# A step of the products between any two engines' parts of a layer norm, in seven of the twelve

## What is computed

```python
x <- LN0(alpha*x + 0.5*SwiGLU_1(x))
x <- LN1(alpha*x + Mix_l(x))          # layer 0: attention || retention; layer 1: S5 state-space model
x <- LN2(alpha*x + 0.5*SwiGLU_2(x))

def layer_norm(x, g, b):
    mu = jnp.mean(xf, -1, keepdims=True)
    var = jnp.mean(jnp.square(xf - mu), -1, keepdims=True)
    return (xf - mu) * lax.rsqrt(var + LN_EPS) * g + b

def swiglu(x, w_gate, w_up, w_down):
    return (jax.nn.silu(x @ w_gate) * (x @ w_up)) @ w_down
```

## Time and profile before

| | us |
|---|---|
| median of 3 runs | 2601.13 |
| lowest and highest | 2600.61, 2606.46 |
| the profiled execution | 2604.88 |
| its span, first to last instruction | 2603.2 |
| mean granted TensorE clock in it | 0.975 of full |

### The profile page before, as it was taken

How to read it: one execution, slowest core, us unless ns; L and a number is a source line. 1 busy time by engine, 2 the same in 40 slices (tenths; PEclk the granted TensorE clock), 3 DMA queues, 4 the chain that set the end, 5 groups by cost and what they waited for, 6 DMA issues and landing times.

```text
span 2603.2 us, 45460 instructions
## 1 busy us (share of the span) xinstructions
PE 2446.0 (94%) x18347; PEld 2295.4 (88%) x18347; DVE 1638.9 (63%) x2564; ACT 1085.3 (42%) x1645; POOL 470.4 (18%) x544
## 2 busy tenths in 40 slices
PE   6998899999899799999999999999999989989998
PEld 6998798998798667779889999999999888989997
DVE  5887766656765445567676657457656675577555
ACT  3433345333544223353254433555433536354333
POOL 5878600002100021200110202021001010121000
PEclk8999999999999999999999999999999999999999
DMA  7667666444354687644456455554555556545553
GB/s 173 175 188 196 164 194 194 131 117 121 114 151 120 211 250 234 172 120 134 119 155 186 149 155 174 173 170 137 155 153 146 170 171 200 154 139 154 147 153 93
DMA packets 676274, 417.26 MB, mean 160 GB/s; under 512 B 31554, under 2 KB 639682, under 8 KB 676066
## 3 DMA queue, kind: packets, MB, share of 16 engines
q1 hardware_dynamic: 669538, 393.98, 52.6%
q0 software_dynamic: 6528, 20.37, 2.6%
HBM read 395.51 MB, written 18.78 MB: 159 GB/s over the span
## 4 chain that ended last, share of the span: by engine, by line
PE 71%; DVE 15%; ACT 4%; issue 4%; DMA 2%; POOL 2%; SPq 1%; POOLq 0%; DVEq 0%; ACTq 0%
PE ps L256 19%; PE ps L257 18%; PE ps L258 18%; DVE w_lo L251 4%; ACT w_hi L242 2%; PE ps L864 2%; PE ps L865 2%; PE ps L866 2%; PE ps L2224 1%; PE ps L1559 1%; DVE h_lo L427 1%; PE ps L1574 1%; PE ps L1052 1%; DVE rstd L512 1%; PE ps L1601 1%
## 5 line engine op out<-in xcount | busy, mean ns | idle before, releaser
L251 DVE TENSOR_TENSOR w_lo<-w_raw,w_hi 128x1024 fp32r<-128x1024 f32 (+1 forms) x648 | 829.6, 1286 | 657.5 <-ACT w_hi L242 653.9
L256 PE MATMUL ps<-x_hi,w_hi 128*128 128x256 f32 (+1 forms) x3200 | 969.6, 303 | 51.0 <-DVE w_lo L251 48.2
L257 PE MATMUL ps<-x_lo,w_hi 128*128 128x256 f32 (+1 forms) x3200 | 955.4, 299 | 0.0
L258 PE MATMUL ps<-x_hi,w_lo 128*128 128x256 f32 (+1 forms) x3200 | 955.0, 298 | 0.0
L242 ACT ACTIVATE w_hi<-w_raw 128x1024 fp32r<-128x1024 f32 (+1 forms) x648 | 668.4, 1033 | 498.5 <-PE ps L258 353.1
L256 PEld LDWEIGHTS ps<-x_hi,w_hi 128*128 128x128 f32 x3200 | 615.5, 192 | 69.5 <-DVE w_lo L251 57.2
L257 PEld LDWEIGHTS ps<-x_lo,w_hi 128*128 128x128 f32 x3200 | 615.7, 192 | 1.4 <-issue 0.2
L258 PEld LDWEIGHTS ps<-x_hi,w_lo 128*128 128x128 f32 x3200 | 615.3, 192 | 0.0
L256 PE MATMUL ps<-h_hi,w_hi 128*128 128x256 f32 (+1 forms) x1408 | 425.2, 302 | 9.7 <-DVE w_lo L251 7.4
L257 PE MATMUL ps<-h_lo,w_hi 128*128 128x256 f32 (+1 forms) x1408 | 415.5, 295 | 0.0
L258 PE MATMUL ps<-h_hi,w_lo 128*128 128x256 f32 (+1 forms) x1408 | 415.2, 295 | 0.0
(11 more groups left out here) (263 smaller groups left out, 2282.8 us busy)
## 6 DMA issues: line engine op xcount, KB each, us to landing
w_raw<-in_ffn_w_gate SPq DMA_DIRECT2D x176, 512.0 KB, 4.3
w_raw<-in_ffn_w_up SPq DMA_DIRECT2D x176, 512.0 KB, 3.9
w_raw<-in_ffn_w_down SPq DMA_DIRECT2D x128, 512.0 KB, 3.9
w_raw<-in_w_in_ab SPq DMA_DIRECT2D x56, 512.0 KB, 4.1
w_raw<-in_ffn_w_down SPq DMA_DIRECT2D x64, 384.0 KB, 3.2
arena<-in_cache_v POOLq DMA_DIRECT2D x64, 256.0 KB, 4.4
arena<-in_cache_k SPq DMA_DIRECT2D x64, 256.0 KB, 3.9
w_raw<-in_w_out_ab SPq DMA_DIRECT2D x16, 512.0 KB, 3.7
```

What stands on the lines that cost most here:

```text
L251: dve.tensor_tensor(T.w_lo[:, u % RING, 0:n], T.w_raw[:, u % RAW, 0:n], T.w_hi[:, u % RING, 0:n].bitcast(F32), ALU.subtract).then_inc(T.w_ ...
L256: pe.matmul(out, w_hi, m_hi, start=first, stop=False)
L257: pe.matmul(out, w_hi, m_lo, start=False, stop=False)
L258: return pe.matmul(out, w_lo, m_hi, start=False, stop=last)
```

## The change

`Norm` takes a number `slack`. With 0 everything stays at its step; with 1 each engine's part moves one more step away from the part of another engine that it waits for, and the norm has 12 steps: squares and their sums in 2 and 3 (from 1 and 2), variance in 5 (from 4), root in 6 (from 4), reciprocal and scaling in 7 and 8 (from 5 and 6), rounding in 8 and 9 (from 5 and 6), `x_lo` in 9 and 10 (from 6 and 7), bias in 10 and 11 (from 7 and 8). N0A, N1A, N2A, N1B, N4A, N4B and N5A get `slack=1`. `STEPS` itself goes from 10 to 9. Nothing happened in the tenth step, but `norm_and_s5`, `beside_a` and `beside_b` count from `Norm.STEPS - 2`, so the S5 part of both groups begins one norm step earlier, in the product step of the norm's last scaling.

```diff
 class Norm:
-    STEPS = 10
+    STEPS = 9
 
-    def __init__(self, T, g, row, scale, products, alone=False):
+    def __init__(self, T, g, row, scale, products, alone=False, slack=0):
 
-        self.alone = alone
+        self.alone, self.steps, n = alone, self.STEPS + 3 * slack, slack
+        self.square_at, self.var_at, self.root_at = 1 + n, 4 + n, 4 + 2 * n
+        self.scale_at, self.round_at, self.rest_at, self.bias_at = 5 + 2 * n, 5 + 3 * n, 6 + 3 * n, 7 + 3 * n
...
     def vector(self, dve):
         T = self.T
-        for i in range(self.STEPS):
+        for i in range(self.steps):
...
-            if i in (5, 6):
-                for k in range(4 * i - 20, 4 * i - 16):
+            if i in (self.scale_at, self.scale_at + 1):
+                for k in self.half(i, self.scale_at):
...
-            if i in (1, 2):
-                for k in range(4 * i - 4, 4 * i):
+            if i in (self.square_at, self.square_at + 1):
+                for k in self.half(i, self.square_at):
                     act.wait_ge(T.centred.h, self.centred + k + 1)
...
-        N1B = Norm(T, B, 1, 1.0, True)
+        N1B = Norm(T, B, 1, 1.0, True, slack=1)
```

More of the change, by code:

```diff
@@ L468, in __init__, with half @@
             c.take(k) for c, k in ((T.affine_done, KT), (T.x_rounded, split), (T.x_ready, split)))
+    def half(self, i, first):
+        return range(4 * (i - first), 4 * (i - first) + 4)
     def x(self, k):
@@ L491, in tensor @@
                 pe.matmul(self.ps, T.ones[:, :], self.acc, start=True, stop=True).then_inc(T.sum_done.h, 1)
-            if i == 4 and self.alone:
+            if i == self.var_at and self.alone:
                 for k in range(KT):
@@ L496, in tensor @@
                       .then_inc(T.sq_added.h, 1)
-            elif i == 4:
+            elif i == self.var_at:
                 pe.wait_ge(T.sq_added.h, self.sq_added + KT - 1)
@@ L509, in vector @@
                        .then_inc(T.centred.h, 1)
-            if i == 5:
+            if i == self.scale_at:
                 dve.wait_ge(T.rstd_ready.h, self.rooted + 1)
@@ L513, in vector @@
                 dve.wait_ge(T.rstd_ready.h, self.rooted + 2)
-            if i in (5, 6):
-                for k in range(4 * i - 20, 4 * i - 16):
+            if i in (self.scale_at, self.scale_at + 1):
+                for k in self.half(i, self.scale_at):
                     dve.scalar_tensor_tensor(self.x(k), self.x(k), T.ln_gain[:, self.row, k:k + 1], self.rstd,
                                              ALU.mult, ALU.mult).then_inc(T.normed.h, 1)
-            if i in (6, 7) and self.products:
-                for k in range(4 * i - 24, 4 * i - 20):
+            if i in (self.rest_at, self.rest_at + 1) and self.products:
+                for k in self.half(i, self.rest_at):
                     dve.wait_ge(T.x_rounded.h, self.rounded + k + 1)
@@ L540, in scalar @@
                 act.activation(self.rstd, self.root_of, ACT.Sqrt, bias=self.eps).then_inc(T.rstd_ready.h, 1)
-            if i in (5, 6):
-                for k in range(4 * i - 20, 4 * i - 16):
+            if i in (self.round_at, self.round_at + 1):
+                for k in self.half(i, self.round_at):
                     act.wait_ge(T.normed.h, self.normed + k + 1)
@@ L548, in scalar @@
                         act.activation(self.x(k), self.x(k), ACT.Identity, bias=self.bias(k)).then_inc(T.affine_done.h, 1)
-            if i in (7, 8) and self.products:
-                for k in range(4 * i - 28, 4 * i - 24):
+            if i in (self.bias_at, self.bias_at + 1) and self.products:
+                for k in self.half(i, self.bias_at):
                     act.wait_ge(T.x_ready.h, self.ready + k + 1)
@@ L556, in gpsimd @@
         T = self.T
-        for i in range(self.STEPS):
-            if i in (1, 2) and not self.alone:
-                for k in range(max(4 * i - 4, 1), 4 * i):
+        for i in range(self.steps):
+            if i in (self.square_at, self.square_at + 1) and not self.alone:
+                for k in self.half(i, self.square_at):
+                    if k == 0:
+                        continue
                     pool.wait_ge(T.squared.h, self.squared + k + 1)
@@ L2654, in layers @@
         F0A, F0B = Ffn(A, ffn_0, loaded[A], 0), Ffn(B, ffn_0, loaded[B], 0)
-        N0A = Norm(T, A, 0, 2.0, True)
+        N0A = Norm(T, A, 0, 2.0, True, slack=1)
         f0a = parts(F0A, (0, 1, 2), N0A)
@@ L2664, in layers @@
         ret_a = Retain(T, M, A, A.tiles, ZONE + 6144, ZONE + 7168, there + ((T.pa_rested, att_a.rested + 2),), there[1:])
-        N1A = Norm(T, A, 1, 1.0, True)
+        N1A = Norm(T, A, 1, 1.0, True, slack=1)
         OA = Out(T, A, w_out, None, N0A.affine + KT, N1A,
@@ L2669, in layers @@
         F1A = Ffn(A, ffn_1, N1A.ready, N1A.affine + KT)
-        N2A = Norm(T, A, 2, 2.0, True)
+        N2A = Norm(T, A, 2, 2.0, True, slack=1)
         their = T.releases[BANKS[-1]]
@@ L2701, in layers @@
         s5_a = S5Group(T, M, S, A, N3A.affine + KT, free)
-        N4A = Norm(T, A, 4, 2.0, True)
+        N4A = Norm(T, A, 4, 2.0, True, slack=1)
         OA2 = Out(T, A, s5_w_out, s5_w_gate, N3A.affine + KT, N4A, ((S.rested, KT),))
@@ L2709, in layers @@
         s5_b = S5Group(T, M, S, B, N3B.affine + KT, (), s5_a)
-        N4B = Norm(T, B, 4, 2.0, True)
+        N4B = Norm(T, B, 4, 2.0, True, slack=1)
         OB2 = Out(T, B, s5_w_out, s5_w_gate, N3B.affine + KT, N4B, ((S.rested, 2 * KT),))
-        N5A = Norm(T, A, 5, 2.0, False)
+        N5A = Norm(T, A, 5, 2.0, False, slack=1)
         f3a += parts(F3A, (2,), N5A)
         F3B = Ffn(B, ffn_3, N4B.ready, N4B.affine + KT)
-        N5B = Norm(T, B, 5, 2.0, False, True)
+        N5B = Norm(T, B, 5, 2.0, False, alone=True)
         f3b = parts(F3B, (0, 1, 2), N5B)
```

2 lines of the change are left out of this document (1 added, 1 removed).

## The result

The changed kernel took 2583.35 us, the median of 5 runs (2577.47 to 2588.54), beside 2604.85 for the kernel before in 5 runs: 0.992 of it, 95% interval 0.990 to 0.994. That is 21.5 us less. In a second series of 5 runs it took 2579.14 us beside 2605.1 (0.9905, interval 0.989 to 0.992), some 25 us less. The forecast was 20.8 us less, and 2580.3 us because it was counted from the first three runs of the kernel before, whose median was 2601.13. The profiled execution of after, 2577.47 us, is the fastest of its five, so a comparison of the two traces shows more than the medians: 27.4 us.

The account below looks back on a forecast made before the run. TensorE, busy 94%, was held to lose time only to holes, chiefly waits for VectorE's weight rests, and low-clock stretches; norm gains plus S5's 2.5 made 20.8 us, from 2601.13 to 2580.3, range 2569 to 2592.

Parts of the forecast that it names:

- The ping-pong: At norms, ScalarE's queued rounding waits for VectorE's scaling, delaying weight rest and TensorE; L251 waits total 55.6 us.
- One sign: In the new profile, ScalarE's idle time ahead of squares and of `x_hi` nearly goes; 5.52 us stood before scaling at N1B.
- N1B, 2.9 us kept: At N1B, of 6.0 us of waits, 0.7 stays at first and 0.7 in each of three down steps.
- N4B, 6.15 us kept: At N4B, of 8.1 us, four waits totalling 4.75 stay, plus 1.4 from GpSimd's additions.
- GpSimd's part of it: At N4B, scaling beside GpSimd's additions takes 2.41 instead of 1.94 us; three times 0.47 makes 1.4 more.
- N2A, 3.55 us kept: At N2A, of 5.3 us, 0.35 stays at the first section and a new 3.2 wait at the third tile.
- N1A, 0.7 us kept: At N1A, of 2.6 us in both transpose waits for ScalarE's move, 0.35 stays each time.
- N3A, 1.0 gained and S5 of group A 2.0: First transposes fill N3A's 1.78 us hole, gaining 1.0; group A's S5 wait falls from 5.5 to 3.5.
- N4A and N5A, 0.6 each: Waits of 0.63 us at N4A and about 0.6 at N5A go, gaining 0.6 each.
- Group B's S5 part, 0.5 lost: Two more scan steps beside down steps, with less room than gate/up steps, lose 0.5 us; bounds 1 gained to 3 lost.
- The clock: Low-clock stretches of 1.5 us each go at N0A, N1A, N1B, N4B; at N2A 2.1 lost becomes 1.5.
- the holes come back: Rival: VectorE's operations run longer than counted, N1B keeps 6 and N4B 8.1; gain 11 us, 2590 us; chance 0.24.

Follow-up runs that it names:

- the rounding alone: Kernel before, with only rounding, `x_lo` and bias one step later in the seven norms, S5 at its old step; 2582.63 us, 0.9906.
- the squares alone: Kernel before, with slack only ahead of the squares in the seven norms, later stages shifted along, S5 at its old step; 2588.89 us, 0.994.
- the mixed version: Changed kernel with N2A's slack (1, 0, 3), N1B's and N4B's scaling through bias over four steps, S5 earlier for group A only; 2572.44 us, 0.9864.

## Why the prediction was right, and where it was not

**What went right.** The ping-pong was the cause: a rounding of ScalarE in the scaling's own step holds back the next weight piece. With the scaling in the same place and ScalarE's rounding in that step, VectorE stands for 1.57 us at N1B and TensorE for 2.56; with the rounding in the next step VectorE does not wait and TensorE stands for 0.89. Where no `x_lo` moves along, the same step gained 2.1 us at N5A and closed both holes at N3A and at N3B. The two kernels differ by 18 us in all, of which `x_lo`'s place has a part. The S5 hole of group A was put at 3.5 us and is 3.57; TensorE's and ScalarE's rows there in the changed kernel, to be held against the earlier trace rows:

```profile
1588.93 1.41 PE L2233 MATMUL ps<-arena 128*32 128x128 f32 x14 [3.57 <-ACT arena L2271]
```

```profile
1587.09 1.70 ACT L2271 ACTIVATE arena<-arena 64x128 f32<-64x128 f32 x4 [7.60 <-DVE arena L2412]
```

ScalarE now waits for VectorE's end (L2412), where it waited for GpSimd's: VectorE is what is late next, as the count said. The two waits of N1A's transposes are 0.7 us, as counted, and N2A has the new wait for its third tile (2.7 where 3.2 was counted). TensorE's waits for L251 at N1B and N4B fell from 14.1 to 6.3 us (9 were forecast), in holes of 1.2 us and less. One sign came out otherwise: ScalarE still waits 2.85 us ahead of the first `x_hi` at N1B, where 5.52 stood and next to nothing was forecast; the weight piece that VectorE takes then was rounded ahead of it.

**Where it was luck.** The sum of 20.8 us lies 0.7 from the first measurement, but the second series gave 25, and the two traces are 28.0 and 25.7 us shorter than the one before. By these the sum was some 5 us low. By the table it was too low at N1B (4.6 for 5.9), N4B (3.4 for 4.9), N2A (2.4 for 5.7 and 3.4), N4A and N5A, and too high at N1A (3.4 for 0.7 and 2.9).

**Terms that were mis-sized.**

- N1B, 2.9 us kept: 1.6 measured. The step that failed is "each of the next three down steps has 1.23 + 0.42 + 1.94 = 3.6 us of VectorE's work against 2.9". The rows above have starts at 1335.84, 1337.70, 1338.83 and 1339.16: the loop takes 3.32, because each instruction starts about 0.1 us before the one ahead of it ends. The distance of starts is the price, for VectorE as for TensorE; I had used durations. And a down step takes 3.07 from start to start when it begins behind a hole, not 2.9. So 0.25 for each step, not 0.7. The first wait was 0.9 where 0.7 was counted.
- N4B, 6.15 us kept: 4.7 measured, by the same step (0.95 + 0.41 + 2.42 is 3.55 from start to start) and because a step of 18 matmuls takes 2.4 and not 2.2 when it begins behind a hole. GpSimd's part of it was right.
- N2A, 3.55 us kept: 3.9 measured, but the sizes lie otherwise. The transpose of the first section was to wait 0.35 and waits 1.16, for VectorE and not for ScalarE. The squares' step does this: with the rounding alone the wait is 0.34, with the squares alone 1.15. GpSimd's additions of the squares now lie beside a weight rest and the first tile, which take 0.53 and 0.54 us longer than in the kernel with the rounding alone. VectorE and GpSimd in the changed kernel, then VectorE with the rounding alone:

```profile
1094.11 1.76 DVE L251 TENSOR_TENSOR w_lo<-w_raw,w_hi 128x1024 fp32r<-128x1024 f32 x1 [3.62 <-ACT w_hi L242]
1095.79 1.23 DVE L930 TENSOR_TENSOR arena<-arena 128x512 f32<-128x512 f32 x1
```

```profile
1092.29 4.18 POOL L572 TENSOR_TENSOR acc<-acc,arena 128x256 f32<-128x256 f32 x4 [4.40 <-ACT arena L541]
```

```profile
1094.24 1.23 DVE L251 TENSOR_TENSOR w_lo<-w_raw,w_hi 128x1024 fp32r<-128x1024 f32 x1 [1.73 <-ACT w_hi L242]
1095.38 0.69 DVE L931 TENSOR_TENSOR arena<-arena 128x512 f32<-128x512 f32 x1
```

- N1A, 0.7 us kept: 1.7 measured, with the new wait for `gate`, which the count did not have.
- N3A, 1.0 gained and S5 of group A 2.0: of N3A's 1.78 two holes of 0.95 and 0.54 are left, so only 0.3 went, and the S5 wait gave its 1.9; with the low stretches the piece is 4.2 and 5.8 us shorter in the two traces.
- N4A and N5A, 0.6 each: 1.2 to 1.3 each in the table. Matmul by matmul, the hole of 0.63 at N4A cost 0.9 us from start to start, and a second one of 0.12 us one down step later, too short for the list of waits, cost 0.4. So each hole cost nearly 0.3 us more than its idle time: the first matmul behind it takes 0.39 to 0.42 instead of 0.28 to 0.31, and the following one starts 0.1 late. I had counted this, and the second hole, at nothing.
- Group B's S5 part, 0.5 lost: 1.1 and 2.0 lost in the two traces, 2.9 with that edit alone. The scan's four holes grew from 10.1 to 10.8 us, and a wait of 1.9 for the first copy is new where 1.4 and 1.4 stood. The wait behind the scan is 5.4 us; with the old step it is 6.2 in the trace of before, but 4.7 in three other traces, so it cannot be said to have fallen. All holes of the piece together are 21.0 and 21.4 us against 21.9 before. The low stretches are longer, 20.5 to 27 us against 17 to 20.5 with the old step, and these two ranges meet: the slack alone, with the S5 part at its old step, also has 20.5 us and lost 0.9. Why the clock falls more often there is not settled.

**The clock.** The sum took one low stretch away at N0A, N1A, N1B and N4B each, and kept one at N2A. At N1A, N1B and N4B none stands in either trace, and the mean granted clock is 0.980 and 0.979 against 0.975. At N0A the first trace has none and the second has one further on, outside the norm; at N2A it is one in one trace and none in the other. Over the whole program low stretches make 129 us before, and 102 and 110 in the two traces of the changed kernel. The two pages divide the gain of the first trace: TensorE's idle time (the span less its busy time) fell from 157.2 to 139.2 us, 18.0, and its busy time, for the same 18347 matmuls, from 2446.0 to 2436.0, 10.0; together they are the difference of the spans. At the 0.43 us that the prediction gave a low us, the 26 us less of low clock make 11. So between a third and two fifths of the gain came through the clock, not far from what the sum had (6.6 of 20.8: four times 1.5, and 0.6 at N2A). But some 7 of the 26 us lie ahead of N0A and behind N5B, where nothing was changed, so a part of this, too, is chance.

**What was not seen.** The prediction priced the first step (squares) and the third (rounding) by the holes they cover at N1B, 2.3 and more. The runs show that they don't add: the squares alone give 16 us, the third step alone 25, all three 22 to 26. At N4B the waits left are 4.9 us with the squares, 6.0 with the third step and 4.7 with all, of 8.1. The likely reason is the middle step: it moved the scaling out of gate/up steps with 1.7 us of room into down steps with 1.2 or less, and with it the squares' 4.9 us at N4B become 5.7 and their 5.9 at N2A 7.1. No kernel had the first and the third step without it at N4B, so this was argued and not shown. At N2A the mixed version had them so, with `x_lo` later still, and the waits of the transposes there fell to 1.4 us. The chance for this, "the holes come back", was put at 0.24, but as something that happens to the whole change, and not as the price of one of its three steps.

## What to carry to other kernels

When one engine's queue carries both a late stage of a side task and the feed of the main task, a stage that waits for its partner's result in the same step holds the feed back; one step of distance takes that wait away. Which of several such steps pays was not what the count said here, so they should be tried one by one, since a step that only moves the work can put it where there is less room. Look also at what comes behind the side task: a longer one can reach into the next part of the main task, as at N1A. Spread what is left over more steps before adding distance. Count an engine's loop from start to start of its instructions, and judge a single hole by its length and not by the low clock that one trace happens to show behind it.
